# Sample attention moved into the prompt jobs of one decoder layer: softmax per sequence, value pages on four column tiles, low weights in the place of raw ones

## What is computed

```python
z = rmsnorm(x) @ w_in                 # q, k, v of both head groups, and 8 forget gates
# diff group: 4 heads, rotated q1,q2,k1,k2 (64 each), v 128
a = softmax(q1 k1^T/8) - lam * softmax(q2 k2^T/8);   oa = a v
# fox group: 8 heads of 64, cf = cumsum(log sigmoid(f + b))
of = softmax(q k^T/8 + cf[t] - cf[s]) v
x = x + rmsnorm(concat(rmsnorm(oa)*(1-lam_init), of) @ w_o)
c = causal depthwise conv (width 3) of g = rmsnorm(x) @ w_gate
x = x + rmsnorm((gelu(c) * (rmsnorm(x) @ w_up)) @ w_down)
# for the sample tokens k, v and log f are the eight gathered pages followed by the new row
```

## Time and profile before

| | us |
|---|---|
| median of three runs | 1682.28 |
| lowest and highest | 1679.20, 1687.02 |
| the profiled execution | 1686.94 |
| its span | 1685.2 |
| TensorE busy | 1530.6 |
| VectorE, ScalarE, GpSimd busy | 718.4, 540.9, 540.1 |

### The profile page before, as it was taken

The page is one execution under the profiler, slowest core; times in us unless marked ns, Lnnn a source line. Parts: engine busy times, 40 slices in busy tenths (PEclk is TensorE's granted clock), DMA queues, the critical chain, the costliest instruction groups (busy, mean ns, idle before and its releaser), DMA issues. The chain is left out here.

```text
span 1685.2 us, 24613 instructions
## 1 busy us (share of the span) xinstructions
PE 1530.6 (91%) x9608; PEld 1347.6 (80%) x9608; DVE 718.4 (43%) x1244; ACT 540.9 (32%) x1072; POOL 540.1 (32%) x328
## 2 busy tenths in 40 slices
PE   3999887899999975867998999999999999999995
PEld 3989776777787743216777999999999999999994
DVE  4421668666544553005544242433423424334245
ACT  4643545544544440005433322031121211312212
POOL 2212334345433322002222433252341422423214
PEclk9999989999999986999999999999999999999997
DMA  5111424354444391992132211121110211211024
GB/s 176 39 39 40 125 88 126 114 157 146 140 126 151 102 320 55 311 324 78 66 98 71 73 53 38 38 63 38 51 57 20 76 37 40 63 38 38 18 84 153
DMA packets 154257, 163.13 MB, mean 97 GB/s; under 512 B 19472, under 2 KB 106512, under 8 KB 154104
## 3 DMA queue, kind: packets, MB, share of 16 engines
q1 hardware_dynamic: 154142, 161.57, 30.1%
HBM read 144.41 MB, written 17.21 MB: 96 GB/s over the span
## 5 line engine op out<-in xcount | busy, mean ns | idle before, releaser
L1149 PE MATMUL PS<-ht_hi,wgu_hi 128*128 128x344 f32 x1056 | 339.3, 321 | 1.1 <-PEq L1230 1.1
L1149 PE MATMUL PS<-ht_lo,wgu_hi 128*128 128x344 f32 x1056 | 338.9, 321 | 0.0
L1149 PE MATMUL PS<-ht_hi,wgu_lo 128*128 128x344 f32 x1056 | 338.8, 321 | 0.0
L472 POOL TENSOR_TENSOR k_page<-k_page,q_bc 128x1024 f32<-128x1024 f32 x64 | 154.8, 2423 | 243.5 <-DMA k_page<-in_cache_fox_k 195.6
L1176 POOL TENSOR_TENSOR wgu_lo<-wgu_raw,wgu_hi 128x1024 fp32r<-128x1024 f32 x44 | 105.6, 2402 | 343.2 <-ACT wgu_hi L1172 343.1
L1693 DVE SCALAR_TENSOR_TENSOR conv<-gate,conv_consts,conv 128x1024 f32<-128x1024 f32 x44 | 79.9, 1817 | 308.7 <-ACT conv L1636 307.9
L817 PE MATMUL PS<-ht_hi,w_hi 128*128 128x344 f32 x576 | 199.1, 346 | 10.8 <-DVE ht_lo L653 10.8
L1149 PEld LDWEIGHTS PS<-ht_hi,wgu_hi 128*128 128x128 f32 x1056 | 200.2, 190 | 1.2 <-issue 1.1
L1149 PEld LDWEIGHTS PS<-ht_hi,wgu_lo 128*128 128x128 f32 x1056 | 199.9, 189 | 0.0
L1149 PEld LDWEIGHTS PS<-ht_lo,wgu_hi 128*128 128x128 f32 x1056 | 199.4, 189 | 0.0
L817 PE MATMUL PS<-ht_lo,w_hi 128*128 128x344 f32 x576 | 189.5, 329 | 0.0
(11 more groups left out here) (217 smaller groups left out, 2497.7 us busy)
## 6 DMA issues: line engine op xcount, KB each, us to landing
k_page<-in_cache_diff_k SPq DMA_DIRECT2D x64, 256.0 KB, 2.6
k_page<-in_cache_fox_k SPq DMA_DIRECT2D x64, 256.0 KB, 2.9
v_page<-in_cache_diff_v SPq DMA_DIRECT2D x64, 256.0 KB, 3.5
v_page<-in_cache_fox_v SPq DMA_DIRECT2D x64, 256.0 KB, 4.2
w_raw<-in_w_in SPq DMA_DIRECT2D x24, 512.0 KB, 4.5
wgu_raw<-in_w_gate SPq DMA_DIRECT2D x22, 512.0 KB, 3.8
wgu_raw<-in_w_up SPq DMA_DIRECT2D x22, 512.0 KB, 3.9
wd_raw<-in_w_down SPq DMA_DIRECT2D x44, 256.0 KB, 2.8
```

The source lines that it names most:

```text
L472: pool.tensor_tensor(kpage[:, J % 2, :], kpage[:, J % 2, :], qbc[:, :], ALU.mult).then_inc(mult_done, 1)
L1149: ins = pe.matmul(PS[:, bank, 0:THIRD], w[:, slot, k, :], a[:, k, i * THIRD:(i + 1) * THIRD], start=(k == 0 and n == 0), stop=(k == KC - 1 ...
```

## The change

The work of decode() moves into project's jobs, sequence by sequence; decode() returns at once.

- k_job and v_job give each page its job. Three key pages are multiplied and reduced ahead of job 0, the other 61 come in jobs 0 to 52, eight in seven jobs. Value pages come from job 8 on, again eight in seven jobs, the last eight two by two in jobs 57 to 60.
- After a sequence's last key page VectorE takes the maxima over its pages (page_maxima), TensorE turns them ("mt"), VectorE takes the maximum of each row (row_maximum), TensorE spreads it ("nm"), VectorE subtracts it (shift), ScalarE takes the exponentials, VectorE the sums, one step a job. scores has three slots.
- value_page(g) takes four matmuls of 256 columns with a stationary of 4 columns, onto partitions 0, 32, 64 and 96 of bank 7. Chunks have bank 6 alone from the jobs on. The eight pages of a sequence are summed there, copied to o_part and stored to od_dram.
- Two slots for value pages: page g is issued in the job of page g-2, after it is used.
- The gate pages are loaded in the projection stage, 13 ahead of each of the tiles 3 to 7; the suffix sums are three matmuls in tile 9, the sums over later pages seven small additions on GpSimd.
- w_raw and w_lo share two slots; load_w waits until the tile two before is used up. Tiles of the jobs are loaded at t = 3 and 7, split at 1 and 5.
- k_rows holds half a unit and is stored at t = 3 and t = 4; the second copy waits for the first store.
- rope multiplies by the cosine in place, after the swap.
- The new token's share, the coefficients and the mixing are small steps on 8 partitions in jobs 60 to 64 and, on GpSimd, after them (eight steps in all). w_o comes in three parts instead of two. merge only has other places for some buffers.

```diff
-    w_raw = view(place.at(o, "w_raw", KC * P), k=KC, n=P); o += 4 * KC * P
+    w_raw = view(place.at(o, "w_raw", 2 * KC * P), s=2, k=KC, n=P)
+    w_lo = view(place.at(o, "w_lo", 2 * KC * P, F32R), s=2, k=KC, n=P); o += 8 * KC * P
     w_hi = view(place.at(o, "w_hi", 2 * KC * P, F32R), s=2, k=KC, n=P); o += 8 * KC * P
-    w_lo = view(place.at(o, "w_lo", 2 * KC * P, F32R), s=2, k=KC, n=P); o += 8 * KC * P
+    vt = place.at(o, "v_t", TOK); o += 4 * TOK
+    k_rows = view(place.at(o, "k_rows", SEQ // 2), t=NT // 2, n=P); o += 2 * SEQ
...
+    k_job = lambda g: (g - EARLY_PAGES) * 7 // 8
+    v_job = lambda g: 8 + g * 7 // 8 if g < 7 * PAGES else 57 + (g - 7 * PAGES) // 2
+    k_pages = lambda J: [g for g in range(EARLY_PAGES, DB * PAGES) if k_job(g) == J]
+    v_pages = lambda J: [g for g in range(DB * PAGES) if v_job(g) == J]
+    ready = lambda b: k_job(PAGES * b + PAGES - 1)
+    at_job = lambda J, lag: [b for b in range(DB) if ready(b) + lag == J]
+    LS, ML = ready(DB - 1) + 6, NJ - 3
+
+    def soft_at(J):
+
+        return ([("mt", b) for b in at_job(J, 2)] + [("nm", b) for b in at_job(J, 3)]
+                + [("ls",)] * (J == LS) + [("ml",)] * (J == ML))
...
+    def z_bank(c):
+
+        return 6 + c % 2 if c < chunk_of(MAPS + 2, 0) else 6
...
             def load_w(n):
-                if n:
-                    sp.wait_ge(w_lo_done, n)
+                if n >= 2:
+                    sp.wait_ge(chunk_done, chunk_of(n - 2, 2) + 1)
                 c = tile_columns(*TILES[n])
-                sp.dma_start(w_raw, w_v[:, :, c:c + P]).then_inc(w_in, 16)
+                sp.dma_start(w_raw[:, n % 2], w_v[:, :, c:c + P]).then_inc(w_in[n % 2], 16)
...
+            load_w(2)
+            sp.wait_ge(pt_in, 16)
+            sp.wait_ge(cid_done, 1)
+            for n in range(3, FT + 4):
+                for g in range(13 * (n - 3), min(13 * (n - 2), DB * PAGES)):
+                    page = sp.value_load(ptab[0:1, g:g + 1], min_val=0, max_val=NPOOL - 1)
+                    sp.dma_start(lf[:, g, :], io["c_lf"][bass.ds(page * P, P), :]).then_inc(lf_in, 16)
                 load_w(n)
...
+                b = g // PAGES
+                if b and g % PAGES == 0:
+                    sp.wait_ge(mult_done, g)
+                    sp.dma_start(qbc[:, :], io["qs_dram"][b:b + 1, :].to_broadcast([P, 2 * GRP])).then_inc(qbc_in, 16)
+
+            def load_value_page(g):
+                if g >= 2:
+                    sp.wait_ge(v_used, g - 1)
+                page = sp.value_load(ptab[0:1, g:g + 1], min_val=0, max_val=NPOOL - 1)
+                for kind, cache in enumerate((io["c_dv"], io["c_fv"])):
+                    sp.dma_start(vpage[:, g % 2, kind * GRP:(kind + 1) * GRP], cache[bass.ds(page * P, P), :]).then_inc(v_in[g % 2], 16)
+
+            wait_evacuated(sp, ("qs", 1))
+            sp.dma_start(io["qs_dram"], q_rows[0:DB, :]).then_inc(qs_stored, 16)
+            load_key_page(0)
+            load_key_page(1)
+            sp.wait_ge(qs_stored, 16)
+            sp.dma_start(qbc[:, :], io["qs_dram"][0:1, :].to_broadcast([P, 2 * GRP])).then_inc(qbc_in, 16)
+            load_w(MAPS + 2)
+            load_key_page(2)
+            load_w(MAPS + 3)
...
-                if t == 0:
-                    sp.wait_ge(mult_done, J)
-                    sp.dma_start(qbc[:, :], io["qs_dram"][u:u + 1, :].to_broadcast([P, 2 * GRP])).then_inc(qbc_in, 16)
                 if J == 0:
-                    load_key_page(0)
-                if J + 1 < NJ:
-                    load_key_page(J + 1)
-                if t in (1, 5):
-                    n = k_tile(u + 2) + (t == 5)
-                    if n < len(TILES):
-                        load_w(n)
+                    for g in k_pages(0):
+                        load_key_page(g)
+                for g in k_pages(J + 1):
+                    load_key_page(g)
+                n = {3: k_tile(u + 2), 7: k_tile(u + 2) + 1}.get(t, len(TILES))
+                if n < len(TILES):
+                    load_w(n)
...
-                if t == 5:
-                    wait_evacuated(sp, ("k", u, 1))
-                    sp.dma_start(kv_out("k", u)[:, columns(u)].rearrange("(t p) c -> p t c", p=P), k_rows).then_inc(k_stored, 16)
+                if t in (3, 4):
+                    h = t - 3
+                    wait_evacuated(sp, ("k", u, h))
+                    sp.dma_start(kv_out("k", u)[h * 512:h * 512 + 512, columns(u)].rearrange("(t p) c -> p t c", p=P), k_rows).then_inc(k_stored, 16)
+                for b in range(DB):
+                    if v_job(PAGES * b + PAGES - 1) + 1 == J:
+                        sp.wait_ge(od_evac, b + 1)
+                        sp.dma_start(od_dram[b], o_part[:, :]).then_inc(od_stored, 16)
+                for g in range(DB * PAGES):
+                    if (v_job(g - 2) if g >= 2 else v_job(0) - 2) == J:
+                        load_value_page(g)
...
             def split_lo(n):
                 pool.wait_ge(w_hi_done, n + 1)
-                pool.tensor_tensor(w_lo[:, n % 2, :, :], w_raw, w_hi[:, n % 2, :, :].bitcast(F32), ALU.subtract).then_inc(w_lo_done, 1)
+                pool.tensor_tensor(w_lo[:, n % 2, :, :], w_raw[:, n % 2, :, :], w_hi[:, n % 2, :, :].bitcast(F32), ALU.subtract).then_inc(w_lo_done, 1)
...
+            def multiply(g):
+                if g % PAGES == 0:
+                    pool.wait_ge(qbc_in, 16 * (g // PAGES + 1))
+                pool.wait_ge(kp_in[g % 2], 32 * (g // 2 + 1))
+                pool.tensor_tensor(kpage[:, g % 2, :], kpage[:, g % 2, :], qbc[:, :], ALU.mult).then_inc(mult_done, 1)
+
+            for g in range(EARLY_PAGES):
+                multiply(g)
             for J in range(NJ):
                 u, t = unit(J), tile(J)
-                n = k_tile(u + 1) + 1 if t == 0 else k_tile(u + 2)
-                if t in (0, 4) and n < len(TILES):
+                n = {1: k_tile(u + 1) + 1, 5: k_tile(u + 2)}.get(t, len(TILES))
+                if n < len(TILES):
                     split_lo(n)
-                if t == 0:
-                    pool.wait_ge(qbc_in, 16 * (u + 1))
-                pool.wait_ge(kp_in[J % 2], 32 * (J // 2 + 1))
-                pool.tensor_tensor(kpage[:, J % 2, :], kpage[:, J % 2, :], qbc[:, :], ALU.mult).then_inc(mult_done, 1)
+                for g in k_pages(J):
+                    multiply(g)
...
-                    if u:
-                        act.wait_ge(k_stored, 16 * u)
-                    dst = k_rows[:, 4 * h:4 * h + 4, :]
+                    if u or h:
+                        act.wait_ge(k_stored, 16 * (2 * u + h))
+                    dst = k_rows
...
+                for b in at_job(J, 4):
+                    act.wait_ge(shifted, b + 1)
+                    wait_evacuated(act, ("nm", b))
+                    act.activation(scores[:, b % 3], scores[:, b % 3], ACT.Exp).then_inc(e_done, 1)
...
+                for b in at_job(J, 5):
+                    sums(b)
+                for g in k_pages(J - 1):
+                    reduce_page(g)
+                for b in at_job(J, 1):
+                    page_maxima(b)
...
+                    if (n, i) == (MAPS + 1, 1):
+                        pe.wait_ge(const_in, 32)
+                        pe.wait_ge(after_step, PAGES)
+                        pe.wait_ge(lfn_in, 16)
+                        dst = bank(("fb",))
+                        pe.matmul(dst, suffix[:, :], lf.rearrange("p g m -> p (g m)"), start=True, stop=False)
+                        pe.matmul(dst, ones_sq[:, :], lf_after.rearrange("p b n m -> p (b n m)"), start=False, stop=False)
+                        pe.matmul(dst.rearrange("p (b n m) -> p b n m", b=DB, m=MAPS), ones_sq[0:1, :],
+                                  lf_new[0:1, :].rearrange("p (b n m) -> p b n m", b=DB, n=1).to_broadcast([1, DB, PAGES, MAPS]),
+                                  start=False, stop=True).then_inc(x_done, 1)
...
+            def value_page(g):
+                b, n = divmod(g, PAGES)
+                pe.wait_ge(v_in[g % 2], 32 * (g // 2 + 1))
+                if n == 0:
+                    pe.wait_ge(e_done, b + 1)
+                    if b:
+                        pe.wait_ge(od_evac, b)
+                for k in range(2):
+                    for half in range(2):
+                        r, c = 64 * k + 32 * half, k * GRP + half * (GRP // 2)
+                        ins = pe.matmul(PS[r:r + 4, 7, 0:GRP // 2], scores[:, b % 3, k, n, 4 * half:4 * half + 4], vpage[:, g % 2, c:c + GRP // 2],
+                                        start=n == 0, stop=n == PAGES - 1, skip_group_check=True)
+                ins.then_inc(v_used, 1)
...
                 if 2 <= J < NJ + 2:
                     weighted_sum(J - 2)
+                if J < NJ:
+                    for e in soft_at(J):
+                        soft(e)
+                    for g in v_pages(J):
+                        value_page(g)
...
 def decode(nc, io, place):
 
-
-    ident = place.at(R_ID, "ident", P)
...
+    return
```

459 lines of the change are left out of this document (236 added, 223 removed).

## The result

| | before | changed |
|---|---|---|
| median (runs) | 1684.61 us (4) | 1747.37 us (4) |
| lowest to highest | 1679.2 to 1687.02 | 1740.02 to 1750.18 |
| profiled execution, its span | 1686.94, 1685.2 | 1750.18, 1748.2 |
| TensorE's granted clock, mean | 0.967 | 0.939 |

The ratio is 1.037, 95% interval 1.0327 to 1.0414. Forecast were 1687 us and a range of 1642 to 1725: the time lies 60 us above the one and 22 above the other. The stage of its own did disappear, and 184 us came in where 121.5 had been reckoned.

A forecast was written before the change was run, and what follows sets the result against it. The job stage was taken as TensorE's, except in units 0 to 2 and 7. Terms -117.0 + 10 + 38 + 9 + 43 + 21 + 8 - 9 + 1.5 = +4.5 on 1682.3 gave 1687 us, range 1642 to 1725.

The forecast's parts named there:

- The queue on SyncE: Job stage: second value pages of six jobs, and page 2 in job 9, wait behind key loads: +43 us.
- half a buffer: Units 0 to 3: ScalarE's second key-row copy waits for the first half's store: +21 us (0 to 35).
- clock: TensorE: eleven waits of 4 us and more at some 2 us each, less existing slow stretches: +8 us (0 to +20).
- projection stage: Projection: gate-page lookups on SyncE delay weight tiles, 7 us, and suffix sums take 2.9: together +10 us.
- value pages, TensorE: TensorE in the jobs: 64 value pages at 0.75 us each, 48 us.
- of it hidden: Units 1 and 2: their idle time covers about 10 us of the value pages' matmuls, leaving +38.
- small steps: Jobs: sixteen transposes and broadcasts of maxima on TensorE, 5 us, and VectorE's work, 4: +9 us.
- unit 7: Last unit: no key pages, so the DMA share falls and it needs 50 instead of 64.8 us; with two waits, -9.
- The first, the waits absorbed: Job stage: VectorE's reductions run ahead and the half buffer is stored in time: 1642 to 1650 us, chance 0.22.
- The second, tiles in turn: Value-page groups: the four column tiles take turns, 1708 us at 1.08 a page, 1780 at 2.2; chance 0.15.
- The third, the low clock after waits: TensorE: a stretch at 1.2 GHz follows every wait above 3 us: +15 on the sum, 1702 us, chance 0.13.
- a landing wait in another job: Sign of a wrong forecast: waits for value pages to land in jobs other than 15, 22, 29, 36, 43, 50.

The follow-up runs named there:

- e2: The changed kernel with the weight-tile load and row stores ahead of each job's key-page loads, value loads still behind them: 1710.71 us.
- Experiment 4: The changed kernel with only each doubled job's second key page issued later, at the end of the job whose reduction frees its buffer: 1716.11 us.
- e3: The changed kernel with the key-page loads behind everything else that a job issues on SyncE: 1651.96 us.
- e1: The changed kernel with the value-page loads ahead of the key-page loads in each job's part of SyncE's program: 1703.23 us.
- d2: The changed kernel with 26 dummy matmuls on TensorE ahead of the second value page's wait in jobs 15, 22, 29, 36, 43 and 50: 1732.77 us.
- e8: e3 plus later third-early-page reduction, gate batches behind tiles, doubled jobs' second key page in its own job, value loads right behind row stores: 1642.0 us.

## Why the prediction was off, point by point

The steps that failed are three terms of the sum, and they are one mechanism. "The queue on SyncE" (+43) counted what stands behind a key load only for the value pages; "half a buffer" (+21) saw a key load before the store in unit 3 alone; and "clock" (+8) priced single restarts and not the idle time in all. The runs showed in their place 97.3 us more idle time of TensorE in the job stage (61.0 for value pages, 29.0 more for key rows, 9.9 for a weight tile, 12.0 less for VectorE's weights, and small ones) and 21 us more of busy time for unchanged matmuls; putting the key loads last in each job takes 95.4 us away again.

| step | forecast | what the traces and runs show |
|---|---|---|
| decode stage goes | -117.0 | gone: VectorE's last write 825.73 to 826.02, the next stage at 827.60 |
| projection stage | +10 | +15.9 (172.2 to 188.15): idle time +7.4 (waits for tiles 9.8), suffix sums 2.9, slower work 5.7 |
| value pages, TensorE | 48 | 44.6 busy, of it 5 at the low clock; 0.55 a page else |
| of it hidden | -10 | -12 (waits for VectorE's weights 20.4 to 8.4) |
| small steps | +9 | 6 busy, and some waits of 0.2 to 0.5 |
| queue on SyncE | +43 | value waits 61.0 (55 without unit 7), and 9.9 for a weight tile |
| half buffer | +21 | key-row waits +29.0; alone, in the kernel before, waits +15.1 and time +20 in units 0 to 3; waits +4 to +6 with the stores ahead of the key loads |
| clock | +8 | old work in the job stage +21, value pages 5, projection some 5 |
| unit 7 | -9 | +10.7, of it value pages' matmuls 6.5: +4 |
| GpSimd's tail | +1.5 | 1.6 (826.02 to 827.60) |
| later stages | 0 | -4.0 |

**The queue on SyncE: right mechanism, too small and too narrow.** TensorE waits for the second v_page in the six jobs named, by 6.3 to 9.3 us. The wait named for page 2 in job 9 isn't in the changed kernel's trace, but only because the wait for the weight tile hides it: in e2 it is 7.7 us, 5 forecast. The chain of job 15 ran as written: from the end of the weighted sum (355.05) to the reduction (359.4), the key pair, the lookup, the value page at 361.7, there at 366.2. That is 11.2 us after the sum against 10.45 forecast, since it landed in 4.1 and not 3.5. The six jobs are longer by 64.5 us, 10.7 each; without their two pages 9.5, against 7. What failed is the list of those who stand behind the key load. I followed the value page to the end, and for the key rows I had unit 3's case alone; but the weight tile of job 7 stands there too, and ScalarE's split of it is the first thing in job 9. My own rule, that every instruction behind a waiting one counts, was applied to one queue item and not to each. Experiment 4 shows the second part of the same error: I took ordinary key loads for harmless, and they are so only when nobody behind them is in a hurry. That unit 0 grew by 18.8 us is in part this: its key-row waits are 9.5 us, and 2.4 in e3. e3's unit 0 is 12.8 us shorter, but with the same code it varies by 5.8 from trace to trace. By the runs the order on SyncE is worth 95 us; forecast were 43 + 21 + 8, and of those the half buffer keeps a part in any order (4 to 6 us of waits).

**The half buffer: right in kind, too small in units 0 to 2.** In job 28 TensorE waits for ScalarE's key rows for 11.1 us, 9 forecast; the store was issued at 492.53, behind a key load, and ScalarE's copy came at 497.67. In units 4 to 6 nothing, as forecast; e1 shows that in units 4 and 5 it was hidden behind the value page, as the prediction had said of unit 4 only. In units 0 to 2 the waits are 24.4 us (21 more than before) against 12: the store was to go out 1.3 us after the sample rows', with no key load before it. In unit 0 the copy ends at 227.79; SyncE waits for a reduction until 228.74, issues the key pair (230.13), waits with the next sequence's query for GpSimd's product until 231.95, issues the weight tile and the sample rows, and the store goes out at 233.81, 6.0 us after the copy. It lands at 240.44, and the four first-half stores of units 0 to 3 take 4.2 to 6.6 us to land, where perhaps 4 had been reckoned. It is mostly the order again: with e2 the waits are 11.4 instead of 36.2.

**The clock: the term that was most wrong in proportion.** I priced only the restart after waits of 4 us or more, 2 us each, and subtracted from it. The cost of a wait was right (1.5 to 2.4 each in d2, which fills the waits in part), but the number of waits wasn't the measure: with 97 us more of idleness, much of the work between waits is at the low level as well. The groups by line of the changed kernel's job stage (count, busy us, mean ns, idle before):

```profile
L1037 PE MATMUL PS<-ht_hi,w_hi 128*128 128x344 f32 x336 | 122.6, 365 | 5.3 <-ACT z_raw L627 5.1 <-ACT v_t L637 0.2
...
L1110 PE MATMUL PS<-k_t,q_t 64*128 64x512 f32 (+3 forms) x384 | 96.7, 617 | 0.0
...
L1194 PE MATMUL PS<-v_page,scores 128*4 128x256 f32 x512 | 44.6, 427 | 61.0 <-DMA v_page<-in_cache_fox_v 61.0
```

The same 384 score matmuls were busy for 84.9 us before and are for 96.7 now. By windows of one line each, the projection's matmuls took 187.9 and take 194.4, the turns 71.7 and 75.5, the weighted sums 78.5 and 77.7: 21 us for work that hasn't changed. It isn't the value groups' doing: in e3, which has them too but half the idle time, these groups together are at 425.0 us, against 444.2 in the changed kernel and 422.8 before. I had carried the old clock of 0.94 over to units that were to idle far more; it came out at 0.83 to 0.85.

**The value pages: right, and better than taken.** 0.75 a page was the guess between 0.54 and 1.08; measured are 0.55, and 0.42 for a second one in a row, what 256 columns cost on the full width (0.43). Four column tiles overlap in full. The Trainium skill's rule (TensorEngine Tiling (Array Packing), Theoretical Speedup, up to 4x at 32 or less) agrees; that a change of mode drains TensorE (Key Properties) can hide only in the 0.13 us between the two numbers. The sum by that rule was 13 lower, and indeed busy time is below the 48.

**Unit 7: wrong.** I took its 15.7 us of idle time for the work of the DMA share of 0.78. The share fell to 0.39 and the idle time rose to 21.4. Of it 8.0 us are the last jobs' weighted sums that wait for VectorE's copies (7.9 before), as the pipeline of jobs runs empty, and 5.8 are for value pages; the rest is small waits. A high share beside idleness isn't its cause until a wait names it.

**The projection stage: nearly right.** Tile 3's raw part was issued at 73.86 (76 forecast) and held TensorE up by 5.2 us; the tiles behind it by 1.0 and 3.6, against 3.3, though at 94 and 109 us and not at 130 and 144. Idle time grew by 7.4 us in all (28.8 to 36.2) and busy time by 8.6 (143.4 to 151.9), of it 2.9 for the suffix sums; the other 5.7 is the old work at a clock of 0.93 instead of 0.96.

**The rivals.** The first, the waits absorbed at 1642 to 1650, describes e3 (1652) and e8 (1642). I gave it 0.22 for the reason that VectorE might run ahead, and no run shows that it does. What brought those times was another order of issues, and the order was written in the kernel. The second, tiles in turn, is refuted. The third, the low clock after waits, was true but was a case with 15 us of its own instead of a term of the sum that grows with each other wait. That is also why the range failed: its top of 1725 was one mishap above the forecast, and what happened is that the queue, the buffer and the clock were all priced too low together, because they are one mechanism. Of the signs named ahead, a landing wait in another job (8, 2.3 and 1.1 us) and projection and job stages together 184.5 us longer instead of 120 said so at once.

**What stays open.** The later stages gave back 4.0 us with unchanged code; no run asks why. How the 21 us of clock divide among the waits was tried for six waits only. What of unit 0's growth belongs to the order and what to the one execution isn't separated.

## What to carry to other kernels

On a queue that issues in program order, list for each waiting instruction everything behind it up to the next job, with the engine that needs it first; put what waits longest last. A wait that is taken away can uncover another that it hid, so remove suspected waits together and not only one by one. Sum the idle time that a change adds before pricing the clock: here 97 us of it brought some 26 us of slower work with them, and dummy matmuls in six waits brought back 9 to 15. When terms of a sum share a cause, widen the range by their sum.
